# First block's attention on TensorE's full array, two heads at a time, with the query tile ahead of the gate tile

## What is computed

```
q, k, v, gate = split(h @ w_in)                 # 32 query heads, 4 key heads, 64 wide
q = rms_norm(q, q_gain); k = rms_norm(k, k_gain)
s = einsum('bqhgd,bkhd->bhgqk', qj, kb) * scale + bias      # keys: block j-1 and block j
s = where(valid, s, -inf)
m = maximum(max(s), sink)
p = exp(s - m);  p = p / (sum(p) + exp(sink - m))
o = einsum('bhgqk,bkhd->bqhgd', p, vb)
return (o * silu(gate)) @ w_out
```

## Time and profile before

| | us |
|---|---|
| median of 3 runs | 2140.9 (2138.85 to 2141.0) |
| span of the profiled execution | 2143.7 |
| PE busy, whole span | 2046.1 (95%) |
| DVE busy, whole span | 959.9 (45%) |
| ACT busy, whole span | 818.2 (38%) |
| first block's units, first statistics matmul to the first output matmul | 123.50 to 699.55 |
| mean granted clock of TensorE | 0.975 |

### The profile page before, as it was taken

One profiled execution on the slowest core, in us unless ns is written; L12 is line 12 of the kernel. 1 busy time (PEld: TensorE's weight loads), 2 busy tenths in 40 slices (PEclk: granted clock), 3 DMA queues, 4 the chain that ended last, 5 costly groups with the idle time before them and its releaser, 6 DMA issues.

```text
span 2143.7 us, 29175 instructions
## 1 busy us (share of the span) xinstructions
PE 2046.1 (95%) x10202; PEld 1568.0 (73%) x10202; DVE 959.9 (45%) x2191; ACT 818.2 (38%) x1907; POOL 42.0 (2%) x61
## 2 busy tenths in 40 slices
PE   4999999999998999689999999999999999988998
PEld 3766666666665787468878888787888878766876
DVE  4255555555555422244454545444444544444222
ACT  4244444444444322243433535244343534334221
POOL 1000000000000000000000000000000000000000
PEclk9999999999998999879999999999999999999999
DMA  6831222222220444502222222222222222203443
GB/s 155 192 100 52 68 59 70 64 69 64 64 69 0 127 128 117 153 25 79 79 59 70 68 78 59 59 78 61 76 78 59 59 78 61 76 20 96 130 117 108
DMA packets 285382, 172.92 MB, mean 81 GB/s; under 512 B 23105, under 2 KB 278113, under 8 KB 284785
## 3 DMA queue, kind: packets, MB, share of 16 engines
q1 hardware_dynamic: 278144, 146.31, 25.4%
q0 software_dynamic: 7168, 25.82, 4.4%
HBM read 156.92 MB, written 14.66 MB: 80 GB/s over the span
## 4 chain that ended last, share of the span: by engine, by line
PE 76%; DMA 12%; DVE 4%; issue 3%; ACT 3%; SPq 2%; DVEq 0%; ACTq 0%; POOL 0%
PE G L436 55%; DMA raw<-in_w_out 4%; DMA raw<-in_swa_w_out 4%; PE S L503 4%; PE O L522 3%; PE S L670 2%; PE T L512 2%; DMA rel_rows<-relb 2%; DVE wl L1143 2%; PE O L743 1%; PE S L715 1%; PE O L687 1%; ACT wh L807 1%; PE S L462 1%; PE T L661 1%
## 5 line engine op out<-in xcount | busy, mean ns | idle before, releaser
L436 PE MATMUL G<-xh,wh 128*128 128x512 f32 (+1 forms) x2624 | 899.5, 374 | 17.3 <-DVE wl L1143 12.6
L436 PE MATMUL G<-xl,wh 128*128 128x512 f32 (+1 forms) x2624 | 845.6, 354 | 0.0
L436 PE MATMUL G<-xh,wl 128*128 128x512 f32 (+1 forms) x2624 | 842.1, 353 | 0.0
L1143 DVE TENSOR_TENSOR wl<-raw,wh 128x512 fp32r<-128x512 f32 x528 | 352.8, 688 | 715.3 <-ACT wh L807 706.7
L436 PEld LDWEIGHTS G<-xh,wh 128*128 128x128 f32 x2624 | 465.8, 190 | 148.1 <-issue 60.4
L436 PEld LDWEIGHTS G<-xh,wl 128*128 128x128 f32 x2624 | 462.2, 189 | 70.5
L436 PEld LDWEIGHTS G<-xl,wh 128*128 128x128 f32 x2624 | 462.5, 189 | 62.5 <-issue 6.5
L807 ACT ACTIVATE wh<-raw 128x512 fp32r<-128x512 f32 x528 | 312.5, 620 | 241.1 <-DMA raw<-in_w_out 106.7
L1047 ACT ACTIVATE att<-att,st 128x144 f32<-128x144 f32 (+3 forms) x64 | 36.9, 576 | 193.3 <-DVE wmeta L1391 103.5
L908 ACT ACTIVATE pT<-T 128x256 f32<-128x256 f32 (+1 forms) x128 | 45.6, 357 | 165.4 <-PE T L512 165.4
L897 ACT ACTIVATE p<-sc,st 128x256 f32<-128x256 f32 (+1 forms) x128 | 61.5, 480 | 93.3 <-DVE st L1206 92.3
(11 more groups left out here) (183 smaller groups left out, 1627.3 us busy)
## 6 DMA issues: line engine op xcount, KB each, us to landing
raw<-in_w_in SPq DMA_DIRECT2D x56, 1024.0 KB, 6.6
raw<-in_swa_w_in SPq DMA_DIRECT2D x16, 1024.0 KB, 5.6
raw<-in_swa_w_in POOLq DMA_DIRECT2D x16, 1024.0 KB, 7.3
raw<-in_swa_w_out SPq DMA_DIRECT2D x16, 1024.0 KB, 7.0
raw<-in_w_out SPq DMA_DIRECT2D x16, 1024.0 KB, 7.3
raw<-in_w_in POOLq DMA_DIRECT2D x8, 1024.0 KB, 7.5
rel_rows<-relb SPq DMA_DIRECT2D x1, 6128.0 KB, 35.9
mixed<-in_x SPq DMA_DIRECT2D x4, 1024.0 KB, 9.9
```

Source lines behind the costliest of these rows:

```text
L436: mm = pe.matmul(d, w[:, slot, k, :], v[:, k, a:b], start=(k == 0 and n == 0), stop=(k == KC - 1 and n == 2))
L1143: V.tensor_tensor(wl[:, slot, q, :], raw[:, slot, q, :], wh[:, slot, q, :].bitcast(F32), ALU.subtract).then_inc(w_lo, 1)
```

## The change

The query block of a unit is split into a rounded part and a rest, stacked on 128 partitions (`qs`: head 0 rounded over rest, head 1 rest over rounded). The keys are split as well, each part stored twice over (`kh2`, `kl2`), by ACT and DVE in place of the DMA copy. A score of one head is two fp32r matmuls over all 128 rows. Values are stored twice side by side (`v2`), and one f32 matmul of 256 columns (both heads' probabilities) serves two heads; its output has each head in its own half of the rows. Transposes of both heads share one bank.

The steps go by query block j: scores at 5, 7, 9, 11, transposes at 8, 10, 12, 14, values at 9, 11, 13, 15. The query tile is now first (slot 0), the gate tile second, and steps 0 to 7 of a unit run beside its own gate tile, steps 8 to 15 beside the next unit's query tile. After the last unit only steps 8 to 15 are left. `gate_exp` and `gate_finish` stand at step 8. PSUM bank `G[:, 0]` holds the query, `G[:, 1]` the gate. In the diff below, the first `swa_step` is ACT's, the lines behind `swa_scale` are of DVE's `swa_step`, and the last hunk is the second half of a `swa_window`.

```diff
+        SWA_S = {5: 0, 7: 1, 9: 2, 11: 3}
+        SWA_T = {8: 0, 10: 1, 12: 2, 14: 3}
+        SWA_PV = {9: 0, 11: 1, 13: 2, 15: 3}
...
-            def duplicate(g):
-                pool.wait_ge(kv_n, g + 1)
-                pool.dma_start(kT1[HD:P, g, :], kT1[0:HD, g, :]).then_inc(kv_dup, 16)
...
+            def swa_scores(u, g, j):
                 a, width = (0, P) if j == 0 else (P * (j - 1), 2 * P)
...
+                after(pe, a_neg, 8 * u + 2 * j - 2)
+                for hh in range(2):
+                    q_block = qs[:, hh, P * j:P * j + P]
+                    dst = S[:, j % 2, 2 * P * hh:2 * P * hh + width]
+                    pe.matmul(dst, q_block, kh2[:, g, a:a + width], start=True, stop=False)
+                    mm = pe.matmul(dst, q_block, kl2[:, g, a:a + width], start=False, stop=True)
+                mm.then_inc(a_s, 1)
+
+            def swa_transpose(u, j):
+                after(pe, a_p, 8 * u + 2 * j + 2)
+                after(pe, a_pT, 4 * u + j - 1)
+                dst = G[:, 2, :] if j % 2 else T[:, :]
+                for s in range(1 if j == 0 else 2):
+                    for hh in range(2):
+                        b = 2 * s + hh
+                        mm = pe.transpose(dst[:, P * b:P * b + P], p1[:, 2 * (j % 2) + hh, P * s:P * s + P], ident)
+                mm.then_inc(a_t, 1)
...
                 for s, b in enumerate(blocks):
+                    mm = pe.matmul(dst, v2[:, g, b, :, :].rearrange("p a n -> p (a n)"),
+                                   pT1[:, j % 2, 2 * P * s:2 * P * s + 2 * P], start=(s == 0),
+                                   stop=(s == len(blocks) - 1))
...
             def swa_step(u, g, m):
                 if m == 0:
+                    q_square(u)
+                if m == 2:
+                    q_rstd(u)
+                if m == 4:
+                    q_split(u)
+                if m - 1 in SWA_S:
+                    swa_exp(u, g, SWA_S[m - 1])
+                if m in SWA_T:
+                    swa_pT(u, SWA_T[m])
+                if m == 8:
+                    gate_exp(u)
...
+            def swa_scale(u, j):
+                width = P if j == 0 else 2 * P
+                for hh in range(2):
+                    n = 2 * j + hh
+                    p = p1[:, 2 * (j % 2) + hh, 0:width]
                     after(dve, a_es, 8 * u + n + 1)
...
+                if m in SWA_S:
+                    swa_bias(i, u, g, SWA_S[m])
+                if m - 2 in SWA_S:
+                    swa_scale(u, SWA_S[m - 2])
+                if m == 8:
+                    gate_finish(u)
+                if m in (12, 15):
+                    swa_out(i, u, g, m // 14)
...
+                for m in range(8):
+                    swa_step(i, u, g, m)
+                    if m % 2 == 0:
+                        split(T_UNIT // 2 + u + 1, 0, m // 2)
```

More of the change, by code:

```diff
@@ L297, in unit_loads @@
                 u = 4 * i + g
-                weights(T_UNIT + 2 * u, 0, w1_v, SWA_GATE + P * (4 * g + i))
+                weights(T_UNIT + 2 * u, 0, w1_v, P * (4 * g + i))
                 after(sp, a_neg, 8 * (u - 1))
@@ L506, in swa_transpose, with swa_stat @@
-            def swa_transpose(u, n):
-                if n == 0:
-                    pe.wait_ge(kv_v, KV)
[L509 to L519, removed]
+            def swa_stat(u):
+                after(pe, q_sq, u + 1)
+                after(pe, a_pT, 4 * u)
+                pe.matmul(G[:, 2, :], head_ones, chain_sq[:, 0:TOK], start=True, stop=True).then_inc(q_stat, 1)
@@ L524, in swa_values @@
                 mm.then_inc(a_pv, 1)
             def swa_step(u, g, m):
[L528 to L537, removed]
+                if m == 1:
+                    swa_stat(u)
@@ L548, in swa_window @@
-                for half in range(2):
-                    bank = 2 * (g % 2) + half
-                    after(pe, q_ln if half else g_act, u - 1 if half else 2 * (u - 1))
-                    if isinstance(u, int) and u < 2:
-                        pe.wait_ge(kv_ln, 2 * u + half + 1)
-                    gemm(T_UNIT + 2 * u + half, half, [G[:, bank, :]], PLAIN, lambda p: step(8 * half + p))
+                        swa_step(u - 1, gp, 8 + p)
+                    elif p in (1, 2):
+                        (kv_stat_of if p == 1 else kv_transpose)(KV - 1)
@@ L560, in _ @@
                     swa_window(i, g, attend=True)
-            for m in range(16):
+            for m in range(8, 16):
                 swa_step(4 * UNITS - 1, 3, m)
@@ L787, in unit_loaded @@
             def unit_loaded(u, half):
-                return (q_in, 16 * (u + 1)) if half else (raw_in[0], KV_LOADS + 16 * (u + 1))
+                return (gate_in, 16 * (u + 1)) if half else (raw_in[0], KV_LOADS + 16 * (u + 1))
             def out_loaded(loads, i, slot):
@@ L857, in kv_rstd, with kv_split @@
                 A(chain_rs[:, 0:TOK], chain_rs[:, 0:TOK], ACT.Exp, scale=-0.5).then_inc(kv_rs, 1)
+            def kv_split(g):
+                act.wait_ge(kv_n, g + 1)
+                for half in range(2):
+                    A(kh2[HD * half:HD * half + HD, g, :], qn[0:HD, :], ACT.Copy).then_inc(kv_hi, 1)
             for g in range(KV):
@@ new lines, in swa_pT, with gate_exp @@
+            def swa_pT(u, j):
+                width = 2 * P if j == 0 else 4 * P
+                after(act, a_t, 4 * u + j + 1)
+                after(act, a_pv, 4 * u + j - 1)
+                A(pT1[:, j % 2, 0:width], (G[:, 2, :] if j % 2 else T[:, :])[:, 0:width], ACT.Copy).then_inc(a_pT, 1)
+            def gate_exp(u):
+                after(act, tile_done, T_UNIT + 2 * u + 2)
+                after(act, g_ok, u)
+                A(gate_e[:, :], G[:, 1, :], ACT.Exp, scale=-1.0).then_inc(g_act, 1)
@@ new lines, in swa_bias @@
+            def swa_bias(i, u, g, j):
+                width = P if j == 0 else 2 * P
+                if j == 0:
+                    after(dve, bias_in[g % 2], 16 * (2 * i + g // 2 + 1))
+                    after(dve, sinku_ok, u + 1)
+                after(dve, a_s, 4 * u + j + 1)
+                after(dve, a_t, 4 * u + j - 1)
+                for hh in range(2):
+                    n = 2 * j + hh
+                    V.tensor_copy(st1[:, n, 5:6], sink_u[:, g % 2, 0, hh:hh + 1])
+                    V.tensor_tensor_reduce(p1[:, 2 * (j % 2) + hh, 0:width], S[:, j % 2, 2 * P * hh:2 * P * hh + width],
+                                           bias[:, g % 2, hh, 2 * P - width:2 * P], -HD ** -0.5,
+                                           sink_u[:, g % 2, 0, hh:hh + 1], ALU.add, ALU.min,
+                                           st1[:, n, 0:1]).then_inc(a_neg, 1)
```

241 lines of the change are left out of this document (126 added, 115 removed).

## The result

The changed kernel takes 2176.54 us in the median of four runs (2174.81 to 2178.47), beside 2140.95 (2138.85 to 2143.97) for the kernel before: ratio 1.0164, 95% interval 1.0151 to 1.0177. The direction was forecast; of 35.6 us the forecast had 15.

What follows compares the result with a forecast made beforehand. TensorE bounds the old kernel; waits on DVE's queue were to cancel its saving: period 36.2 us plus 1.2 for clock, 37.4. With start, loop turns and end, the output block comes 15 us later: 2156 us, range 2130 to 2176.

Steps and rivals of the forecast that it cites:

- the bound moves to DVE's queue: Units' attention: TensorE waits for DVE's scales, 1.2 us before first transposes, 4.9 before second, 0.35 before third.
- the period without clock: One query-and-gate period: chain 11.47, projection 18.2, attention 6.2 and third wait 0.35 give 36.2 us against 36.49.
- the query chain: ACT and DVE work from statistics to first scores: about 6.5 us, equal to TensorE's own, so no wait.
- Rival 4: Query chain in each period is late too: 0.5 to 1 us a period, time 2168; chance 0.12.
- the clock term: Half-clock work behind the second transposes' pause: 1.2 us net a period, bounds 0 and 3.
- rival 3: Behind the pause, short waits make half clock last two stretches: period 39.2 us, time 2183; chance 0.10.
- loop turns 2.9 as before: Units' loop: its turns add 2.9 us to the 15 periods of the stage.
- Start and end: Around the 15 periods: statistics at about 116.0 us, projection resumes at 126.2, last unit's end takes 24.6.
- early gate load: Start: gate weights asked for where the query's were, over 10 us ahead of use; no cost counted.
- Rival 2: Units' stage: TensorE stays the bound, period 29.9 us, time 2043; chance 0.13 with cases up to rival 1.

Runs made afterwards that it cites:

- run with fill and no loop: Changed kernel with 18 useless 512-column matmuls ahead of each unit's second transposes and the units' loop written out: 2134.2 us, ratio 0.9958.
- fill run: Changed kernel with 18 useless fp32r matmuls of 512 columns ahead of each unit's second transposes, loop kept: 2150.21 us, ratio 1.0035.
- spread version: Changed kernel with sigmoid on ACT, gate work spread over steps 9 and 11, scale ahead of bias, loop written out, first gate load held: 2066.16 us.
- scales first: Changed kernel with DVE's scale of block j put ahead of the bias of block j+1, nothing else: 2162.69 us, ratio 1.0089.

## Why the prediction was wrong in size

**Right: the bound moves to DVE's queue.** 2.53 us to the first transposes (2.62 forecast), 8.88 to the second (8.85), pauses of 0.98 and 4.77 (1.2 and 4.9), 0.16 before the third (0.35). The placement run shows it directly: gate work moved behind scale 1, and 44.6 us come back, the clock's part included.

**Right: the period without clock.** 36.2 was worked out; 36.27 stands in the run with fill and no loop. Against 36.49 the saving is gone, as forecast.

**Right: the query chain.** 6.76 us from statistics to scores for 6.5; its wait is at most 0.2. Rival 4 falls.

**Wrong: the clock term, "1.2 net a period".** With the loop written out it fits one half-clock stretch: a steady period is 37.55, against 36.27 with fill, 1.28 more. In the changed kernel itself one stretch costs 1.5, and nine of 15 periods had two. Two stretches were rival 3, at 39.2 a period (38.8 to 39.0 measured), but not for its reason: no short wait stands inside the 6.8 us, which begin 1.0 to 3.9 us before the pause is over. The fill run prices the term at 24.3 us in the stage; 15 times 1.2 is 18.

**Wrong: "loop turns 2.9 as before".** This is the step that failed most. In the old stage TensorE is the bound, and the written-out loop gives 3.0 of the stage. In the new one the chain through DVE is the bound, and DVE's turn lies in it (the row at 560.12): the pauses at the turns are 7.84 instead of 4.77, and half-clock work follows them even under the fill. The two turns cost 9.7 us under the fill (41.1 us twice for 36.27). Another 3.9 are in the ten other periods of the loop's body, which are 36.55 to 36.85 under the fill and 36.27 with the loop written out; the first three periods, which stand ahead of the loop, are 36.2 to 36.3 in both runs. In the body each wait is about 0.1 longer; that this is the engines' handling of register addresses is argued, not shown.

The forecast stage was 15 x 37.4 + 2.9 = 563.9 us; 581.80 were measured, 17.9 more. By the runs, in this order: chain, 543.96 for 543, +1; loop (557.49 less 543.96), 13.5 for 2.9, +10.6; clock, 24.3 for 18, +6.3.

The two losses share a part, so the order matters somewhat: taken the other way (loop first, 16.4), the clock is 21.5. With either order the loop is the larger miss.

**Start and end.** Statistics came at 117.69 for 116.0. The early gate load, which the prediction took as harmless, delayed the first query weights (7.9 us to land, then 5.6 once the gate load was held back). From the last statistics to the output block it took 32.84 us; 34.8 were in the sum (6.5, the 3.7 to the resumed projection, 24.6). The two misses, 1.7 late and 2.0 early, nearly cancel, by luck. The time itself misses by 20.5 us (2176.54 for 2156), 2.5 more than the span: the prediction took 2.8 off the span for the median, as in the kernel before, and here they differ by 0.3.

**Rival 2**, TensorE as the bound, was true of a kernel one could have had. Its 29.9 us was too low: in the spread version TensorE is busy for 31.04 in a period of 31.98. That is still 4.5 below the old period, so the dense forms do save. The Trainium skill (TensorEngine Tiling (Array Packing), Key Properties) says that a change of tiling mode drains TensorE. The traces agree in the direction, but the runs don't tell the drain from the shorter matmuls.

**What stays open:** why some periods get one half-clock stretch, others two, and others with an equally long pause none. The written-out loop has one in each steady period, the loop with scales first has two in each.

## What to carry to other kernels

Before packing work more densely on the fullest engine, read which helper's queue its next input stands in, and put long passes (here a 3.35 us reciprocal) behind the pieces that the full engine waits for; that one line was worth 2%. When the bound passes from a full engine to a chain of waits, loop turns and clock stretches are on the path that were free or cheap before, so carry neither term over from the old profile: look which engine's turn stands in the chain, and next to which piece.

## What the hardware showed unexpectedly

- More matmuls made the kernel faster: 18 useless ones a unit took 26.3 us off, with the granted clock at 1.00 in 13 of 15 periods.
- A pause of 2.24 us left the clock at 1.00 in one kernel, a pause of 2.29 us in another was followed by 3.4 us at half, and in the first kernel one pause of 2.25 us was so too, among others as long that were not.
- `Ln` and `Exp` on ACT take 1.3 us for 128x512, add and reciprocal on DVE 3.8.
- A turn of the loop kept DVE from its next instruction for 3.1 us. It cost TensorE about 1.5 us where TensorE was the bound, and 3.07 us more pause where DVE's queue was.
- Fewer waits did not mean more clock: with scales first, the `T` waits went, and the mean clock of every steady period was 0.91.
- The Trainium skill (TensorE: Matmul & The Clock Gate, HAM oscillation) describes pauses that recur in each turn of a loop and the clock that falls each time. The changed kernel's trace agrees in that all 15 periods have a stretch at half clock, and the fill run shows the size, 1.62 us a period. With shorter pauses it was not each time: 3 of 15 periods with the sigmoid on ACT.
